# Output projection computed as columns with its weights stationary, in a one-core decoder step on Trainium2

## What is computed

```python
h = rmsnorm(x, attn_norm_w)
proj = h @ w_in                      # short convolution and windowed attention follow, gated
merged = sigmoid(g_conv) * y_conv + sigmoid(g_attn) * y_attn
x = x + merged @ w_out               # the output projection, 1024 x 1024
h2 = rmsnorm(x, ffn_norm_w)
logits = h2 @ w_router + b_router    # 32 experts
top_vals, top_idx = top_k(logits, 4); gates = softmax(top_vals)
# for each expert e: u = xs @ w_up[e] + b_up[e]; a = swiglu(u); y += gate * (a @ w_down[e] + b_down[e])
x = x + y
```

## Time and profile before

| | us |
|---|---|
| median of 3 runs | 1147.54 |
| lowest and highest | 1146.79, 1148.38 |
| span of the profiled execution | 1145.4 |
| PE busy in the span | 1097.6 (96%) |
| DVE busy | 437.5 (38%) |
| ACT busy | 188.0 (16%) |
| mean rate of all DMA | 388 GB/s |

### The profile page before, as it was taken

The page is one execution under the profiler, slowest core; times in us unless marked ns, Lnnn a source line. Parts: engine busy times, 40 slices in busy tenths (PEclk is TensorE's granted clock), DMA queues, the critical chain, the costliest instruction groups (busy, mean ns, idle before and its releaser), DMA issues.

```text
span 1145.4 us, 15065 instructions
## 1 busy us (share of the span) xinstructions
PE 1097.6 (96%) x6055; PEld 497.1 (43%) x6055; DVE 437.5 (38%) x858; ACT 188.0 (16%) x398; POOL 88.4 (8%) x161
## 2 busy tenths in 40 slices
PE   9999999999999999999898999999999999999997
PEld 6689898543333333333333333333333333333332
DVE  4577786753433223233223232323232323232322
ACT  2133341221321101010101010101010101010101
POOL 1785215000000000000000000000000000000000
PEclk9999999999999999999999999999999999999999
DMA  9947629999999999999999999999999999999997
GB/s 313 314 128 186 210 85 353 416 357 425 400 420 426 419 432 431 430 433 431 433 433 429 434 430 433 435 428 434 429 434 431 431 434 429 435 429 434 425 423 287
DMA packets 53206, 444.36 MB, mean 388 GB/s; under 512 B 13101, under 2 KB 19373, under 8 KB 35741
## 3 DMA queue, kind: packets, MB, share of 16 engines
q1 hardware_dynamic: 46712, 435.83, 91.7%
q0 software_dynamic: 5600, 7.32, 2.4%
q10 hardware_dynamic: 852, 0.64, 0.2%
HBM read 439.78 MB, written 2.37 MB: 386 GB/s over the span
## 4 chain that ended last, share of the span: by engine, by line
PE 62%; DMA 37%; DVE 0%; issue 0%; ACT 0%; ACTq 0%; SPq 0%; DVEq 0%
PE pA L2051 32%; PE pB L2051 21%; DMA ring<-in_w_up 21%; DMA ring<-in_w_down 10%; PE pM L2051 6%; DMA area<-in_w_up 5%; PE pM L2054 1%; PE pA L2054 1%; DMA x<-in_x_prompt 1%; ACT area L1269 0%; DVE x L1898 0%; SPq L800 0%; DVE conv_row L1812 0%; DVE area L1973 0%; DVE x L1978 0%
## 5 line engine op out<-in xcount | busy, mean ns | idle before, releaser
L2051 PE MATMUL pA<-ring,hn 128*64 128x512 f32 x1536 | 352.6, 602 | 23.0 <-DMA ring<-in_w_up 23.0
L2051 PEld LDWEIGHTS pA<-ring,hn 128*64 128x64 f32 x1536 | 105.3, 137 | 218.8 <-issue 185.5
L2051 PE MATMUL pB<-ring,area 128*64 128x512 f32 (+2 forms) x784 | 171.5, 591 | 6.6 <-DMA ring<-in_w_down 5.8
L2051 PE MATMUL pA<-area,hn 128*64 128x512 f32 x512 | 119.3, 610 | 10.4 <-DMA area<-in_w_up 10.4
L2051 PE MATMUL pB<-area,ring 128*128 128x132 f32 (+2 forms) x928 | 126.4, 327 | 0.0
L2051 PEld LDWEIGHTS pB<-area,ring 128*128 128x128 f32 (+1 forms) x928 | 106.7, 175 | 18.2 <-issue 2.3
L2051 PEld LDWEIGHTS pB<-ring,area 128*64 128x64 f32 (+2 forms) x784 | 58.5, 136 | 101.2 <-issue 87.8
L1898 DVE TENSOR_TENSOR x<-pM,x 128x512 f32<-128x512 f32 x60 | 40.1, 691 | 147.7 <-PE pM L2051 147.7
L1257 ACT ACTIVATE area<-area 128x512 f32<-128x512 f32 x30 | 18.9, 631 | 385.2 <-DVE area L1881 385.2
L1812 DVE COPY conv_row<-pM 128x512 f32<-128x512 f32 x30 | 20.6, 686 | 146.0 <-PE pM L2051 146.0
L2051 PEld LDWEIGHTS pA<-area,hn 128*64 128x64 f32 x512 | 36.2, 139 | 74.5 <-issue 59.7
(11 more groups left out here) (348 smaller groups left out, 907.1 us busy)
## 6 DMA issues: line engine op xcount, KB each, us to landing
ring<-in_w_up SPq DMA_DIRECT2D x36, 4096.0 KB, 29.8
ring<-in_w_down SPq DMA_DIRECT2D x18, 4096.0 KB, 29.0
area<-in_w_up SPq DMA_DIRECT2D x12, 4096.0 KB, 30.2
ring<-in_w_up SPq DMA_DIRECT2D x16, 2048.0 KB, 13.4
area<-in_w_down SPq DMA_DIRECT2D x6, 4096.0 KB, 30.0
ring<-in_w_in SPq DMA_DIRECT2D x22, 1024.0 KB, 10.0
ring<-in_w_down SPq DMA_DIRECT2D x16, 1024.0 KB, 11.6
ring<-in_w_up SPq DMA_DIRECT2D x16, 1024.0 KB, 8.4
```

The costliest lines, as they stand in the source:

```text
L2051: return pe.matmul(out, w, m, start=start, stop=stop, skip_group_check=True)
```

## The change

The output projection is computed as columns, with 128 x 128 tiles of w_out stationary and tokens moving. First come tokens 128 to 255 together with the 8 samples (`x_out`, 136 columns, in two passes over the eight output tiles: k 0 to 3, then 4 to 7), then tokens 0 to 127 (`y_out`, 128 columns, tile by tile). ScalarE copies the results from PSUM to SBUF as columns. PE transposes them back to rows (`turn_x`, `turn_s`, `turn_y`), and VectorE adds the turned rows from the PM bank to `x`. The router takes the projection's columns alone; the router product of the raw x is made early, in step (3, 1) of the input projection (`xr_groups`), from raw columns that ScalarE keeps, and is added (`x_groups`, `y_groups`). The router weights are scaled by ScalarE (`xr_weights`) and no longer by VectorE in the branch. Squares go to PSUM instead of `hn`. The samples and tokens 128 to 255 are routed first, then tokens 0 to 127. Load 8a no longer waits for the squares, 6a stands before 4, and load 6 is cut at another column.

```diff
-FIRST_ORDER = [0, 1, 11, 2, 3, 10, 7, "8a", 4, "6a", 5, "6b", "refill"]
+FIRST_ORDER = [0, 1, 11, 2, 3, 10, 7, "8a", "6a", 4, 5, "6b", "refill"]
+SIXTH_CUT = 8 * NT - 128
...
+    after[9].append(("xr_weights", 0))
+    after[slot(3, 1)].append(("xr_groups", 0))
...
-BRANCH = [("out", (2, 0)), ("out", (0, 0)), ("x_cols", 0), ("rms", 2), ("out", (0, 1)), ("x_cols", 1), ("logits", 2),
-          ("s_split", 0), ("out", (1, 0)), ("x_cols", 2), ("rms", 0), ("part", (0, 0, 6)), ("groups", 0), ("x_cols", 3),
-          ("logits", 0), ("part", (0, 6, KT)), ("half", 0), ("part", (1, 0, 4)), ("count", 0), ("part", (1, 4, 6)),
-          ("x_cols", 4), ("part", (1, 6, KT)), ("half", 1), ("ahead", 1), ("x_cols", 5), ("rms", 1), ("logits", 1),
-          ("gather", 1), ("count", 1), ("gather", 2)]
...
+BRANCH = [("x_out", 0), ("x_out", 1), ("turn_x", 0), ("y_out", 0), ("turn_x", 1), ("y_out", 1), ("turn_s", 0), ("turn_s", 1),
+          ("rms", 1), ("y_out", 2), ("rms", 2), ("x_groups", 0), ("y_out", 3), ("x_logits", 0), ("y_out", 4), ("s_split", 0),
+          ("y_out", 5), ("turn_y", 0), ("y_out", 6), ("x_count", 0), ("y_out", 7), ("turn_y", 1), ("gather", 0), ("turn_y", 2),
+          ("y_groups", 0), ("gather", 1), ("rms", 0), ("y_logits", 0), ("gather", 2), ("y_count", 0), ("gather", 3)]
+TURNED_TILES = {("turn_y", 0): (0, 4), ("turn_y", 1): (4, 2), ("turn_y", 2): (6, 2), ("turn_x", 0): (0, 4), ("turn_x", 1): (4, 4),
+                ("turn_s", 0): (0, 4), ("turn_s", 1): (4, 4)}
...
-        gathers = [sprobT[:], late[:, D - 128:D]]
+        gathers = [late[:, D - 128:D], sprobT[:]]
...
+        raw_groups = [cst[:, C_BUCKET:C_BUCKET + 128], sprobT[:], top8[:, 0, :]]
...
+        def x_out(t):
+
+            if t < 6:
+                return pA[:, 512 * (t // 3) + 136 * (t % 3):512 * (t // 3) + 136 * (t % 3) + 136]
+            return pB[:, 0, 136 * (t - 6):136 * (t - 6) + 136]
+
+        def y_out(t):
+
+            f = slice(128 * (t // 2), 128 * (t // 2) + 128)
+            return pA[:, 1024:1536][:, f] if t % 2 else pB[:, 1, f]
...
@@ -835,14 +850,13 @@
                 elif j == 7:
                     sp.wait_ge(sig_used, 2 * KT)
                 elif j == "6a":
-                    sp.wait_ge(misc_free, FILL["groups", 0])
-                    sp.dma_start(first_place(6)[:, 0:2 * D], rows_of(3, 0)[:, 0:2 * D]).then_inc(first_loaded[6], 16)
+                    sp.wait_ge(misc_free, FILL["x_groups", 0])
+                    sp.dma_start(first_place(6)[:, 0:SIXTH_CUT], rows_of(3, 0)[:, 0:SIXTH_CUT]).then_inc(first_loaded[6], 16)
                     continue
                 elif j == "6b":
-                    sp.dma_start(first_place(6)[:, 2 * D:4 * D], rows_of(3, 0)[:, 2 * D:4 * D]).then_inc(first_loaded[6], 16)
+                    sp.dma_start(first_place(6)[:, SIXTH_CUT:SLOT], rows_of(3, 0)[:, SIXTH_CUT:SLOT]).then_inc(first_loaded[6], 16)
                     continue
                 elif j == "8a":
-                    sp.wait_ge(norm_sq, 3)
                     sp.wait_ge(stored, 16 * 11)
                     sp.dma_start(hn_flat[:, 0:2 * D], rows_of(4, 0)[:, 0:2 * D]).then_inc(first_loaded[8], 16)
                     continue
...
+            for m in range(2):
+                for h in range(2):
+                    o = 1024 * m + 512 * h
+                    nc.scalar.activation(x_raw[:, 4 * h:4 * h + 4, 128 * m:128 * m + 128],
+                                         pA[:, o:o + 512].rearrange("p (k n) -> p k n", k=4), ACT.Copy).then_inc(raw_kept, 1)
...
+                elif what == "xr_weights":
+                    act.wait_ge(wr_loaded, 32)
+                    act.wait_ge(misc_free, FILL["vectors", 0])
+                    for k in range(KT):
+                        ins = nc.scalar.activation(w_router_sb[:, k, :], w_router_sb[:, k, :], ACT.Copy,
+                                                   scale=cols[:, V_FNORM + k:V_FNORM + k + 1])
+                    ins.then_inc(wr_ready, 1)
...
+                if what == "x_out" and a == 1:
+                    for b, src in enumerate((pA[:, 0:408], pA[:, 512:920], pB[:, 0, 0:272])):
+                        n = src.shape[1] // 136
+                        act.wait_ge(out_full, 3 * b + n)
+                        nc.scalar.activation(hT[:, 3 * b:3 * b + n, 128:], src.rearrange("p (t n) -> p t n", t=n),
+                                             ACT.Copy).then_inc(cols_x, 1)
+                elif what == "y_out":
+                    if a == 0:
                         act.wait_ge(bias_moved, 2 * 16 * BIAS_MOVES)
                         act.wait_ge(moved_by_sync, SYNC_MOVED[-1])
...
+                    act.wait_ge(out_full, KT + a + 1)
+                    nc.scalar.activation(x1_cols[:, a, :], y_out(a), ACT.Copy).then_inc(cols_y, 1)
+                elif what in ("turn_x", "turn_y"):
+                    m = what == "turn_x"
+                    t, n = TURNED_TILES[what, a]
+                    act.wait_ge(misc_free, FILL[what, a])
+                    if (what, a) == ("turn_y", 0):
+                        act.wait_ge(norm_sq, 3)
+                    o = 768 if what == "turn_y" and a == 2 else 512 * (a > 0)
+                    ins = nc.scalar.activation(pA[:, o:o + 128 * n], x[:, m, 128 * t:128 * (t + n)], ACT.Square,
+                                               accum_out=stat[:, 3 * m + a:3 * m + a + 1])
+                    if t + n == KT:
                         ins.then_inc(norm_sq, 1)
...
+                if what in ("turn_x", "turn_y", "turn_s"):
+                    t, n = TURNED_TILES[what, a]
+                    m = ("turn_y", "turn_x", "turn_s").index(what)
+                    xs = x[0:TOK[m][1], m, 128 * t:128 * (t + n)]
+                    V.tensor_tensor(xs, misc_bank()[0:TOK[m][1], 0:128 * n], xs, ALU.add).then_inc(misc_free, 1)
...
+                elif what == "x_groups":
+                    b = misc_bank()
+                    groups_summed(raw_groups[1], b[:, 0:128])
+                    groups_summed(raw_groups[2], b[:, 128:136]).then_inc(misc_free, 1)
+                elif what == "y_groups":
+                    groups_summed(raw_groups[0], misc_bank()[:, 0:128]).then_inc(misc_free, 1)
+                elif what == "x_logits":
+                    b = misc_bank()
+                    dve.wait_ge(rms_ready, norms)
+                    routed(2, b[0:DEC, NE:2 * NE], False)
+                    routed(1, b[:, 0:NE], True)
...
                 elif what == "s_split":
 
-                    V.memset(s_parts[0:96], 0.0)
-                    link(V.memset(s_pos[0:96], -1.0))
-                    dve.wait_ge(bias_moved, 2 * 16 * BIAS_MOVES)
-                    dve.wait_ge(moved_by_sync, SYNC_MOVED[-1])
                     dve.wait_ge(hn_ready, 1)
-                    h_s, r_s, p_s = hn[0:DEC, 2, :], s_rest[0:DEC], s_part[0:DEC]
-                    link(V.tensor_copy(xs_row, x[0:DEC, 2, :]))
+                    h_s, p_s = hn[0:DEC, 2, :], s_part[0:DEC]
                     link(V.tensor_copy(s_parts[0:DEC], h_s))
-                    link(V.tensor_tensor(r_s, h_s, s_parts[0:DEC], ALU.subtract))
-                    link(V.tensor_copy(p_s, r_s))
+                    link(V.tensor_tensor(h_s, h_s, s_parts[0:DEC], ALU.subtract))
+                    dve.wait_ge(s_kept, 1)
+                    link(V.tensor_copy(p_s, h_s))
                     V.tensor_copy(s_parts[32:32 + DEC], p_s)
-                    link(V.tensor_tensor(r_s, r_s, p_s, ALU.subtract))
-                    V.tensor_copy(s_parts[64:64 + DEC], r_s).then_inc(s_parts_ready, 1)
+                    link(V.tensor_tensor(h_s, h_s, p_s, ALU.subtract))
+                    V.tensor_copy(s_parts[64:64 + DEC], h_s).then_inc(s_parts_ready, 1)
                     select(0)
...
-            first_picks(1)
+            first_picks(0)
...
+            def w_out_tile(t, k):
+
+                w = ring[:, place(W_IN_CHUNKS + t // 4), :].rearrange("p (k n) -> p k n", k=KT)
+                return w[:, k, 128 * (t % 4):128 * (t % 4) + 128]
...
+                    pe.wait_ge(sig_used, GATED[LAST, "c21"] if a else GATED[LAST - 1, "c21"])
+                    for t in range(KT):
+                        for k in range(4 * a, 4 * a + 4):
+                            mm = matmul(x_out(t), w_out_tile(t, k), yc[:, k, 128:], start=(k == 0 and t % 3 == 0),
+                                        stop=(k == KT - 1))
+                            if t == k == 0:
+                                mm.then_inc(ring_free, 1)
+                        if a:
+                            mm.then_inc(out_full, 1)
+                elif what == "y_out":
+                    if a >= 2:
+                        pe.wait_ge(cols_y, a - 1)
+                    for k in range(KT):
+                        mm = matmul(y_out(a), w_out_tile(a, k), yc[:, k, 0:128], start=(k == 0 and a < 2),
+                                    stop=(k == KT - 1))
+                        if a == 4 and k == 0:
```

(62 more changed lines are left out.)

263 lines of the change are left out of this document (80 added, 183 removed).

## The result

| | before | after |
|---|---|---|
| median of 6 runs, us | 1147.53 | 1151.02 |
| lowest and highest | 1146.79, 1148.44 | 1149.84, 1152.35 |
| span of the profiled execution | 1145.4 | 1148.0 |
| first up product of pair 0 | 241.25 | 243.21 |
| w_down quarters issued | 242.37 | 244.32 |

The ratio is 1.0026, 95% interval 1.0015 to 1.0036; a second measurement of the changed kernel gave 1.0031 (1.0019 to 1.0043). The change costs about 3 us. That is in the forecast's range and 1.3 us over the forecast itself.

What follows compares the result with a forecast made beforehand. Bound: the expert weight stream, which resumes late by what PE's first up product is late. +1.0 router groups, -3.0 projection, +4.2 waits and steps made +2.15 us, so 1149.7 us; range 1148.5 to 1151.0, with rivals 1146.2 to 1152.8.

Steps and rivals of the forecast that it cites:

- The bound and the rule for the end: Expert weight stream: once it has run dry, the end is late by what PE's first up product is late.
- Ahead of the branch: PE in the input projection: raw router groups add 1.04 us, so the branch starts at 197.9.
- The projection: PE's output projection: 28.8 us instead of 31.8, a gain of 3.0 us.
- the high end of the two that were named and not the proportion: Price of 128-column products: 0.225 us at the high end, 0.4 us more in all; in proportion to columns 0.218, taken.
- The waits: PE in the branch waits for VectorE: 0.9 us before the x logits, 1.9 us before turn_y 1.
- The split: VectorE's split of the sample rows, 5.2 us, ending at 232.1, directly ahead of the add for turn_y 0.
- from these logits to the first up product nothing changes: End of the branch: last logits on VectorE at 237.25, then 6.2 us as before, first up product at 243.4.
- rival 2: PE's wait before turn_y 1 drops its clock to 1.2 GHz: 1.7 us more, up +3.85, 1151.4 us; chance 0.19.
- The queue: SyncE's loads: 4 at 223.7, 6a at 223.0, 5 at 233.3, w_down quarters at 244.5; nothing gained is kept.
- the first hole: Weight stream at 232 to 236 us, 1.3 us lost in the kernel before; expected to shrink by some 0.8 us.
- the second: Weight stream's hole ahead of the w_down quarters, 242 to 245 us, 1.6 us lost before; expected to widen.
- The 2.15 us that I put between the profiled span and the median: Before's median 1147.54 lies 2.15 us over its profiled span; added to the span of 1147.5 to give 1149.7.

Runs made afterwards that it cites:

- a_oldq: The changed kernel with load 4 before 6a again and load 8a waiting for the squares of tokens 0 to 127; 1155.02 us, 1.0053 of before.
- a_again: The changed kernel, unchanged, measured a second time; 1150.88 us, 1.0031 of before.
- a_nosplit: The changed kernel with the split of the sample rows cut to its first cast, second and third parts left out; 1148.16 us, 0.9999 of before.
- a_swap: The changed kernel with load 4 before 6a again and load 8a waiting only for the branch's first squares; 1150.62 us, 1.0020 of before.
- a_move: The changed kernel with gather 1 of y moved behind the y logits' product; 1150.34 us, 1.0027 of before.
- a_pool: The changed kernel with the split of the sample rows moved from VectorE to GpSimd; 1153.73 us, 1.0048 of before.

## Why the prediction came out as it did

**The bound and the rule for the end: right.** What was said of the first up product held for the last add in every kernel with an undisturbed queue, to 0.9 us, and always with that on the late side. The one exception, a_oldq, is where the queue stood for over 12 us.

**Ahead of the branch: +1.04 worked out, +0.57 found** (197.35 against 196.78 on PE's timeline). The groups themselves took 1.0 us, as priced, but PE was already 0.23 us early ahead of them; behind them it was 0.66 late (55.14 against 54.48), and 0.1 of that came back on the way.

**The projection: right for x_out, 0.3 short for y_out.** x_out's 128 passes took 14.83 us, 116 ns each. The tiles of y_out took 1.79 us, 112 ns a pass, the high end of the two that were named and not the proportion. In all 29.2 instead of 28.8. Loads of 128 x 128 weights lie under the passes here too: they are listed with 190 ns each, and a pass takes 112 to 116.

**The waits: right in kind, each too long.** PE waited 0.26 us before the x logits, not 0.9: it came when worked out (222.04, not 222.0), and VectorE's chain earlier. The router groups were added by 222.15 (222.9 worked out). The split ran from 226.28 to 231.48, 5.2 us as priced, but from 0.6 us earlier; the wait before turn_y 1 became 1.26, not 1.9. By the last logits VectorE was 0.8 us ahead of the forecast (236.45, not 237.25). The terms that were too dear are the handshakes and the late start of the branch.

**The step that failed: "from these logits to the first up product nothing changes".** Its length did hold where the clock held (236.34 to 242.30, 6.0 us in a_again). But in before PE worked through that stretch on the gathers of y; in after these stand ahead of it and PE idles 1.48 us. In the profiled execution the clock fell behind that wait and not behind the one named in rival 2, and the stretch took 6.76 us. So the near hit of the first up product, 243.21 instead of 243.4, is luck, two errors that cancel: with the clock held it comes at 242.3, 1.1 us ahead of the forecast, and 0.9 us for the clock were left out.

**Rival 2 had too small a chance.** Of six profiled executions in which PE waited 1.3 us, 1.5 us or both, the clock fell in four (after, a_nosplit, a_swap, a_oldq) and held in two (a_again, a_move). The two rows of before that spoke for and against it were just that, a coin, and I read the one against as the rule. The waits were shorter than the 1.85 us from which the rival said it decides, and the price was 0.9 to 2.5 us instead of 1.7.

**The queue: right.** Load 4 at 223.19, 6a at 222.18, 5 at 232.57, quarters at 244.32 (223.7, 223.0, 233.3 and 244.5 worked out), the first hole smaller, the second wider, nothing kept. Not seen was that 8a's release is needed by the reversed order.

**Around the span.** The 2.15 us that I put between the profiled span and the median were not a property of the kernel: in after, time less span is 1.8 us, and before's profiled execution was a short one, 4.0 us from its last add to its end where a_again has 5.75. The median of after is 3.5 us over before's, its last add 2.2. Of the 1.3 us between them, which are also what the forecast is short by, the spread of single executions may be all, or a loss of after behind the last add a part. That the total lies in the range does not decide it.

## What to carry to other kernels

A cheaper stage pays only through the instruction that lets the next stage's transfers go. Follow each engine's in-order queue to that instruction: here 2.6 us less of PE work in the projection were worth nothing, since a 5.2 us piece of side work on VectorE had lost the PE work that used to hide it. When work is moved ahead of a wait, ask what PE will do during the wait; an idle of 1.3 to 1.5 us may cost the clock too, and one profile of it shows one toss of that coin. And compare the last instruction of the chain as well as the spans, and see whether the medians agree with it.

## What the runs showed of the hardware

- Behind 1.3 to 1.5 us without work PE's granted clock fell to the 1.2 GHz level in some executions and not in others, of the same program too: six of eleven such waits, and none that products filled. Behind 3.29 us it fell at once, twice (sixteen passes 3.76 and 3.40 us instead of 2.03).
- Small VectorE instructions were held for as long as GpSimd's instruction beside them: a product of two masks in SBUF took 2.15 us instead of 0.19, a TENSOR_SCALAR 1.55 instead of 0.24. An idle GpSimd is no free place for side work while VectorE has the critical chain.
- GpSimd took 2.1 us for a float32 subtraction of 8 x 1024 and 1.03 to 1.08 for a cast (a_pool), VectorE 1.21 and 0.67 (after).
